# Hybrid diffusion step on one core: modulation with the conditioning columns stationary, prompt routing inside the latent q and k stage, prompt steps 2.95 gathers apart

## The reference

```
def modulation(cvec, w_ada, b_ada):                 # w_ada: 1024 x 6144 for each layer
    mod = jax.nn.silu(cvec) @ w_ada + b_ada
    return jnp.split(mod[:, None, :], 6, axis=-1)

def trunk_layer(x, mod, lp, l, ctx):
    sh1, sc1, g1, sh2, sc2, g2 = mod
    h = modulate(x, lp['norm1_g'], sh1, sc1)
    y, new_ctx = mixer(h, lp, l, ctx)               # pooling, neighbourhood, conv, differential
    x = x + g1 * y
    h = modulate(x, lp['norm2_g'], sh2, sc2)
    x = x + g2 * peer_ffn(h, ...)
    return x, new_ctx

# peer_ffn, for each token and each of 8 heads:
s = einsum('thpk,hpnk->thpn', qry, sub_keys)        # two rows of 128 scores
s1, i1 = top_k(s[:, :, 0], 16); s2, i2 = top_k(s[:, :, 1], 16)
sc, ci = top_k(all 256 sums s1 + s2, 16)            # "routing": 16 experts of 16384
e, g = expert numbers, softmax(sc)
act = gelu(u_tab[e] . h);  y += (g * act) * v_tab[e]
```

## Time and profile before

| | |
|---|---|
| median of 3 runs | 5567.07 us (5561.44 to 5568.31) |
| profiled execution | 5559.97 us |
| its span | 5558.2 us |
| PE, DVE, ACT, POOL busy | 86%, 60%, 34%, 32% |
| weight load on PE (PEld) | 44% |
| DMA | 1652 MB, mean 297 GB/s |

### The profile page before, as it was taken

One profiled execution on the slowest core, in us unless ns is written; L12 is line 12 of the kernel. 1 busy time (PEld: TensorE's weight loads), 2 busy tenths in 40 slices (PEclk: granted clock), 3 DMA queues, 4 the chain that ended last, 5 costly groups with the idle time before them and its releaser, 6 DMA issues.

```text
span 5558.2 us, 47001 instructions
## 1 busy us (share of the span) xinstructions
PE 4754.9 (86%) x14692; PEld 2460.7 (44%) x14692; DVE 3357.0 (60%) x7181; ACT 1867.9 (34%) x4962; POOL 1760.4 (32%) x1599
## 2 busy tenths in 40 slices
PE   8885999999988778888888789899988777777877
PEld 8684447964434224334554244554334222222222
DVE  0425654147766867766545846577766867667544
ACT  0121023124422334366643311444422333333333
POOL 0200610013222445433333436022322344434432
PEclk9987997579999999999999999999999999999999
DMA  5653221369976999999999923059976999999998
GB/s 178 204 196 96 73 83 59 104 215 349 353 281 258 421 420 410 420 404 384 385 413 420 421 85 106 20 201 348 347 280 233 421 422 421 421 420 416 420 421 359
DMA packets 270202, 1652.11 MB, mean 297 GB/s; under 512 B 31040, under 2 KB 31088, under 8 KB 105472
## 3 DMA queue, kind: packets, MB, share of 16 engines
q0 software_dynamic: 190896, 1365.43, 61.2%
q1 hardware_dynamic: 76032, 276.86, 14.4%
q10 hardware_dynamic: 3024, 6.82, 0.3%
HBM read 1642.16 MB, written 6.82 MB: 297 GB/s over the span
## 4 chain that ended last, share of the span: by engine, by line
PE 43%; DMA 35%; DVE 11%; ACT 7%; issue 3%; POOL 0%; DVEq 0%; ACTq 0%; POOLq 0%
DMA arena<-experts,bsb 26%; PE ps L1619 10%; PE ps L1997 9%; DMA arena<-experts,peidx 9%; PE ps L1609 6%; PE ps L1785 6%; DVE arena L1539 3%; PE ps L1897 2%; PE ps L1875 2%; PE ps L1727 2%; DVE arena L1297 2%; ACT L970 1%; ACT T L974 1%; PE ps L1911 1%; ACT bsb L971 1%
## 5 line engine op out<-in xcount | busy, mean ns | idle before, releaser
L1997 PE MATMUL ps<-arena,T 128*128 128x512 f32 x4096 | 2003.5, 618 | 530.5 <-ACT T L974 529.0
L1539 DVE CUSTOM_DVE_ANT_0 arena<-arena,h_sb 128x1024 f32<-128x1024 f32 x1024 | 1254.2, 1226 | 771.8 <-DMA arena<-experts,bsb 768.0
L631 POOL DMA_INDIRECT arena<-experts,bsb x1024 | 1092.7, 1067 | 1670.3 <-PE ps L1997 1545.9
L1997 PEld LDWEIGHTS ps<-arena,T 128*128 128x128 f32 x4096 | 715.3, 191 | 1736.7 <-ACT T L974 1154.1
L970 ACT ACTIVATE bsb<-T 128x1 f32<-128x1 f32 x1024 | 205.9, 201 | 1321.3 <-DVE T L1539 1320.0
L1619 PE MATMUL ps<-h_sb,wring 128*128 128x128 f32 (+1 forms) x1792 | 509.9, 442 | 96.5 <-DVE h_sb L1334 86.2
L616 POOL DMA_INDIRECT arena<-experts,peidx x256 | 282.2, 1102 | 809.6 <-DVE arena L1297 754.8
L1931 PE MATMUL ps<-h_sb,wring 128*128 128x512 f32 x1024 | 456.9, 599 | 32.8 <-DVE arena L1487 30.3
L974 ACT ACTIVATE T<-ident,bsb 128x128 f32<-128x128 f32 x1024 | 410.9, 401 | 33.5
L1619 PEld LDWEIGHTS ps<-h_sb,wring 128*128 128x128 f32 x1792 | 280.7, 196 | 316.4 <-issue 301.7
L1287 DVE CUSTOM_DVE_ANT_0 arena<-arena,h_sb 128x1024 f32<-128x1024 f32 x256 | 312.6, 1222 | 103.5 <-DMA arena<-experts,peidx 102.6
(11 more groups left out here) (283 smaller groups left out, 4622.9 us busy)
## 6 DMA issues: line engine op xcount, KB each, us to landing
wring<-w SPq DMA_DIRECT2D x528, 512.0 KB, 4.7
arena<-experts,bsb POOLq DMA_INDIRECT x1024, 15.3
bsb<-bias POOLq DMA_DIRECT2D x16, 512.0 KB, 3.9
arena<-subk POOLq DMA_DIRECT2D x4, 1024.0 KB, 7.1
arena<-v_scratch POOLq DMA_DIRECT2D x64, 64.0 KB, 2.1
arena<-experts,peidx POOLq DMA_INDIRECT x256, 7.9
x_sb<-xT POOLq DMA_DIRECT2D x1, 2048.0 KB, 13.7
v_scratch<-arena ACTq DMA_DIRECT2D x8, 256.0 KB, 2.0
```

Source lines behind the costliest of these rows:

```text
L631: gp.indirect_dma_start(rows[:, n % NS, :], None, experts, bass.IndirectOffsetOnAxis(ap=eidx[:, t % 2, i:i + 1], axis=0)).then_inc(row_in[ ...
L1539: v.tensor_tensor_reduce(e, e, htok(t), 1.0, 0.0, ALU.mult, ALU.add, dots[:, t % 2, i:i + 1]).then_inc(dot, 1)
L1997: mm = pe.matmul(ps[:, 6 + half, :], diag[:, n % ND, :], rows[:, n % NS, D + half * 512:D + (half + 1) * 512], start=(i == 0), stop=(i == ...
```

## The change

1. **Modulation.** The conditioning columns become the stationary operand, padded to 32 columns (`csil32`), and the weights move past them, 512 at a time. The chunks of `w_ada` are stored another way (`_row_chunks`): four chunks are one group of 512 output columns, each chunk with a quarter of the rows. The four partial products go to four column groups of the array (partitions 0, 32, 64, 96 of one PSUM bank). ACT copies the bank (`modulation_rows`), and four small matmuls with `pick` (two columns, each with a one for every quarter), add the four quarters and turn the result into columns (`modulation_columns`). There are 12 groups for a layer; those of layer 1 stand at every second nat job.
2. **Prompt routing** of each layer moves into the latent q and k stage of that layer, nine steps behind each `qk_norm`. It has its own scratch and score area. `prompt_gates` and `prompt_soften` go behind the attention.
3. **Spacing.** The steps of the prompt mixer of layer 1 stand 2.95 gathers apart instead of 2.4; the last is at gather 505.

```diff
-NADA = 48
+NADA, ADA_GROUPS = 48, 12
 def gather_of(k):
-    return PAIRS + 12 * k // 5
+    return PAIRS + 295 * k // 100
...
+        pick = sb("pick", [P, 2])
+        lroute, proute = routing(bsb, 256), routing(arena, 26752)
-        pscores = at(arena, 0, 16, NKEYS)
+        pscores = at(arena, 24704, 16, NKEYS)
+        csil32 = at(arena, 28416, KD, 32)
+        mrow = at(arena, 24704, 2, 512)
...
             # ACT
-            act.activation(csil[:], csil[:], ACT.Silu).then_inc(csil_ok, 1)
+            act.activation(csil32[:, :, 0:2], csil[:], ACT.Silu).then_inc(csil_ok, 1)
+            def modulation_rows(l, n):
+                act.wait_ge(ada_row, ADA_GROUPS * l + n + 1)
+                need(act, ada_cols, ADA_GROUPS * l + n - 1)
+                act.activation(mrow[:, n % 2, :], ps[:, 1 + 2 * (n % 2), :], ACT.Copy).then_inc(ada_rows, 1)
...
-            prompt_gates(0)
                 job_out(NJOBS - 1)
+                prompt_gates(l)
...
             # DVE
+            own.link(v.tensor_reduce(pick[:], ident.rearrange("p (q r) -> p r q", r=32)[:, 0:2, :], AX_X, ALU.add))
-            for _ in prompt_route(0):
-                pass
-            prompt_soften(0)
+                routing_steps = prompt_route(l)
                 for n in range(NQ + 1):
                     if n < NQ:
                         qk_mean(n)
                     if n >= 1:
                         qk_norm(n - 1)
+                        for _ in range(9):
+                            next(routing_steps, None)
...
                     job_probs(n)
+                prompt_soften(l)
                 if l + 1 < DEPTH:
                     modulation(l + 1)
...
             # PE
-            def modulation_chunk(l, c):
-                wait_chunk(pe, "A", l, c)
-                for k in range(KD):
-                    mm = pe.matmul(ps[:, 1, 2 * c:2 * c + 2], chunk_of("A", l, c)[:, k * P:(k + 1) * P], csil[:, k, :], ...)
-                mm.then_inc(used("A", l, c), 1)
+            def modulation_group(l, n):
+                need(pe, ada_rows, ADA_GROUPS * l + n - 1)
+                for q in range(4):
+                    wait_chunk(pe, "A", l, 4 * n + q)
+                for kk in range(2):
+                    for q in range(4):
+                        mm = pe.matmul(ps[32 * q:32 * q + 32, 1 + 2 * (n % 2), :], csil32[:, 2 * q + kk, :], chunk_of("A", l, 4 * n + q)[:, kk * 512:(kk + 1) * 512], ...)
+                        if kk:
+                            mm.then_inc(used("A", l, 4 * n + q), 1)
+                for q in range(4):
+                    wait_used(pe, "A", l, 4 * n + q)
+                pe.sem_inc(ada_row, 1)
+            def modulation_columns(l, n):
+                pe.wait_ge(ada_rows, ADA_GROUPS * l + n + 1)
+                for i in range(4):
+                    c = 4 * n + i
+                    mm = pe.matmul(ps[:, 5, 2 * c:2 * c + 2], mrow[:, n % 2, i * P:(i + 1) * P], pick[:], start=True, stop=True)
+                mm.then_inc(ada_cols, 1)
```

More of the change, by code:

```diff
@@ L642, in _ @@
             act.wait_ge(ctab, 16)
-            act.activation(csil[:], csil[:], ACT.Silu).then_inc(csil_ok, 1)
+            act.wait_ge(csil_zero, 1)
+            act.activation(csil32[:, :, 0:2], csil[:], ACT.Silu).then_inc(csil_ok, 1)
[3 more added lines that the diff above has]
+                act.activation(mrow[:, n % 2, :], ps[:, 1 + 2 * (n % 2), :], ACT.Copy).then_inc(ada_rows, 1)
+            for n in range(ADA_GROUPS):
+                modulation_rows(0, n)
             def prompt_mixer(l):
@@ L895, in map_exp @@
                                    bias=st[:, o + i:o + i + 1], accum_out=st[:, o + 2 + i:o + 3 + i]).then_inc(exp_done, 1)
+                ada_job = {NDIFF + 2 * n + 2: n for n in range(ADA_GROUPS)}
                 def job_out(n):
@@ L1005, in _ @@
                     y_out(t)
[L1006 to L1008 removed]
+                if l + 1 == DEPTH:
                     give(NL - 1, NL)
@@ L1027, in modulation, with route @@
                 v.sem_inc(ada_ok, 1)
-            def route(l, sc, eidx_out, gate_out, idx_sem, top_sem, gate_free):
+            def route(l, r, sc, eidx_out, gate_out, idx_sem, top_sem, gate_free):
+                top, topf, topi, csc, ci, abf, sel, half = [r[n] for n in ("top", "topf", "topi", "csc", "ci", "abf", "sel", "ef")]
                 cand = sc.rearrange("p n c -> p (n c)").rearrange("p (h a b) -> p h a b", h=GH, a=TOPK)
@@ L1101, in route, with soften @@
                 yield
[L1103 removed]
+            def soften(r, gates, gexp_sem, n, ok_sem):
                 v.wait_ge(gexp_sem, n)
+                total, inv = r["sums"][:, 0, :], r["sums"][:, 1, :]
                 g3 = gates.rearrange("p (h k) -> p h k", h=GH)
[L1107 to L1109 removed]
+                own.link(v.tensor_reduce(total, g3, AX_X, ALU.add))
+                own.link(v.reciprocal(inv, total))
+                v.tensor_tensor(g3, g3, inv.unsqueeze(2).broadcast_to([P, GH, TOPK]), ALU.mult).then_inc(ok_sem, 1)
             def prompt_mixer(l):
@@ L1430, in _ @@
                         conv_norm()
+                for _ in routing_steps:
+                    pass
                 def map_max(m):
@@ L1567, in _ @@
                     at_dot = gates_at(t)
-                    if t == 0:
-                        steps = itertools.chain(latent_route(0, 1), latent_route(1, 0), latent_route(1, 1))
-                    elif t + 1 < NL:
-                        steps = itertools.chain(latent_route(t + 1, 0), latent_route(t + 1, 1))
-                    else:
-                        steps = prompt_route(l + 1) if later else iter(())
+                    groups = [(0, 1), (1, 0), (1, 1)] if t == 0 else [(t + 1, 0), (t + 1, 1)] if t + 1 < NL else []
+                    steps = itertools.chain(*[latent_route(*tg) for tg in groups])
                     for i in range(PAIRS):
@@ L1576, in _ @@
                         dot_row(t, i)
-                        if t + 1 < NL or here > gather_of(PSTEPS - 1) + 3:
-                            for _ in range((2, 1 + i % 2, 1 + i % 2, 3)[t]):
-                                next(steps, None)
+                        for _ in range(1 + i % 2 if t else 2):
+                            next(steps, None)
                         if i - 4 in at_dot:
@@ L1590, in _ @@
                             next(mixer)
-                    for _ in steps:
-                        assert t == NL - 1
+                    assert next(steps, None) is None
                 assert next(mixer, None) is None
@@ L1760, in prompt_mixer @@
                     yield
-            for c in range(NADA):
-                modulation_chunk(0, c)
             pe.wait_ge(ada_ok, 1)
+            for n in range(ADA_GROUPS):
+                modulation_group(0, n)
+                if n:
+                    modulation_columns(0, n - 1)
+            modulation_columns(0, ADA_GROUPS - 1)
+            pe.wait_ge(ada_ok, 2)
             for _ in prompt_mixer(0):
@@ L1904, in _ @@
                         job_values(n - 1)
-                    if l + 1 < DEPTH and n >= NDIFF:
-                        for c in range(3 * (n - NDIFF) // 2, 3 * (n - NDIFF + 1) // 2):
-                            modulation_chunk(l + 1, c)
+                    if l + 1 < DEPTH and n > NDIFF and (n - NDIFF) % 2:
+                        if (n - NDIFF) // 2 < ADA_GROUPS:
+                            modulation_group(l + 1, (n - NDIFF) // 2)
+                        if 0 < (n - NDIFF) // 2 <= ADA_GROUPS:
+                            modulation_columns(l + 1, (n - NDIFF) // 2 - 1)
                     pe.wait_ge(pd_ready, NJOBS * l + n + 1)
@@ L1915, in _ @@
                 if l + 1 < DEPTH:
-                    pe.wait_ge(ada_ok, l + 2)
+                    pe.wait_ge(ada_ok, l + 3)
                 for h in range(4):
@@ L2035 @@
     order = (0, 2, 1, 3)
-    stream, small, rowg, lamrow = [_col_chunks(a["w_ada"][l]) for l in range(DEPTH)], [], [], []
+    stream, small, rowg, lamrow = [_row_chunks(a["w_ada"][l]) for l in range(DEPTH)], [], [], []
     for l in range(DEPTH):
```

52 lines of the change are left out of this document (23 added, 29 removed).

## The result

The changed kernel takes 5324.04 us (median of 4, 5315.08 to 5333.51) beside 5567.69 us for the kernel before on the same chip: ratio 0.9565, 95% interval 0.9541 to 0.9588. Forecast were 5288 us and faster; the gain is 244 us instead of 279, inside the range.

The account below looks back on a forecast made before the run. Gathers were the largest item in the chain, with PE alone on modulation, DVE alone on routing, and nat jobs at 1.2 GHz. Terms -69 - 40 - 160 - 20 + 10 = -279 us gave 5288 us, range 5230 to 5370.

Parts of the forecast that it names:

- rival 1: Modulation groups: column groups run one after the other at 2.4 GHz, 6.87 us a group; 5352 us in all; chance 22%.
- Rival 4: Both q and k stages: DVE, not PE, sets them, steps stretched to 1.3, and spacing brings nothing; 5332 us; chance 12%.
- A: Layer 0's modulation at the start: becomes bound by the chunk ring, ending at 114 instead of 182.6 us; -69 us.
- B: Layer 0's prompt routing: PE's gap before the latent projections shrinks 49.8 us, q and k holds cost 10; -40 us.
- E: Layer 1: routing in its q and k stage +10, softening at the layer boundary -1, gates behind attention +1; +10 us.
- C: Layer 1's modulation among layer 0's nat jobs: twelve groups at 2.4 GHz, stage about 113 us; -160 us with later waits.
- Rival 2: Nat stage of layer 0: groups run side by side but the clock stays at 1.2 GHz; 5363 us; chance 8%.
- D: Layer 0's expert stage: wider spacing of prompt mixer steps raises the gather rate; -20 us, bounds 0 and -37.

Follow-up runs that it names:

- second fit: Changed kernel with routing steps placed by time budgets per unit, none in unit 6, leftovers behind layer 0's nat jobs and layer 1's last unit; 5304.33 us, ratio 0.9523.
- in pairs: Against the kernel that waits for each chunk by itself: a group's chunks 0 and 1 are finished before chunk 2 begins; 5279.82 us, ratio 0.9498.
- both finds: Changed kernel with each chunk waited for by itself and released early, plus routing steps fitted a third time in both layers; 5250.65 us, ratio 0.9445.

## Why the forecast was right, and where it was off

**What bounds, and the sign: right.** Every stage that was named moved, and those that were not named moved by at most 3.4 us. The four column groups run side by side at 1.92 us (forecast 1.72); one column group costs 7.03 and rival 1 is out. That rival was itself priced too low: I gave it 5352 us, and the kernel that has it takes 5414. Its cycle at the start was 10.1 us at 2.4 GHz, not 9.2, and 11.8 on average, since most of its groups ran in part at 1.2 GHz (7.03 to 9.66 us). The Trainium skill ("TensorE: Matmul & The Clock Gate", Part 3) has 2.38x for three column tiles, 0.79 of ideal; here four reached 7.03/1.92 = 3.7, 0.92 of ideal, and the measurement decides. Rival 4 is out too: the 1024-wide routing steps took 1.21 to 1.23 us, as before (1.22 to 1.23), one of them (at 610.11 us) with POOL at work beside it, and the spacing brought its share.

**A, the start: right, 6 us short.** The cycle is 8.5 us, the end 119.9 instead of 114. I took the middle of a warm and a cold start; it was cold (0.66). That slots released together make the wait is shown from both sides: five slots cost 15.3 us, and waiting for each chunk by itself, which releases the first ones earlier, gives 26.5 back.

**B, the gap: right to 0.3 us** (49.7), and shown again by undoing it (48.8).

**B and E, the hold in the q and k stages: the mechanism right, the size off.** I had 10 us in each layer and measured 15.4 and 19.0. The step that failed is "PE is held 4 us after unit 8 and 6 us at the last two transposes". PE's last two waits were 3.65 + 6.33, 6 us more than before, as forecast, and behind unit 8 it waited 2.43. What I had not seen is another 3.66 at 631.79 us, ahead of unit 8's steps. In the timeline VectorE comes late to the centring of the convolution in unit 6, behind nine steps, ScalarE waits for that, and the next mean waits for ScalarE; in the second fit, with no step in unit 6, this wait is gone. In layer 1 pieces of the projection behind a wait ran at the lower clock too (8.1 and 8.7 us for 7.03). That the place of the steps does it is shown: fitted to the idle time, with 11.3 us of them ahead of the first two units, the same 140 steps cost 1.3 and 2.6 us.

**C, the nat jobs: the step that failed.** The forecast -162 came as -136. The sum, 12 groups at 3.1 us + 0.5 for chunks, holds at 2.4 GHz: groups with their columns take 3.3 us, two jobs and a group 7.4 to 7.6 us. The kernels in which the clock stayed up (in pairs, both finds) had the stage at 112 us; the forecast of 113, less the 5 us ahead of the first group, is 108, and waiting for chunks makes up the rest (9.7 us in pairs, where the sum had 6). What failed is the premise that 2.4 GHz holds, taken from layer 1's jobs, where nothing waits for a chunk. In the profile PE waited 2.1, 0.8 and 1.5 us for chunks, each time the pieces behind the wait went over to 1.2 GHz, the stage had a clock of 0.77, and its last eight jobs cost 13 us more for it. That the clock is the loss is shown by the stage's table. Rival 2, the stage at 1.2 GHz, thus came true in part. That idle time before a group brings the clock down is shown as far as this: in the eight kernels with 4.6 to 14.2 us of it the clock was 0.74 to 0.90, in the five with 0 to 1.4 us 0.91 to 1.00, with the tail at 1.00 in all five. The small columns and the narrow stationary tiles, rival 2's reasons, are excluded as causes by themselves: the kernel in pairs has all of both at 1.00. It is no law: the same code had its tail at 1.2 GHz in one profile and at 2.4 in another, more waiting did not mean a lower clock, the kernel with one column group had two slow groups (8.2 and 8.5 us for 7.05) with no wait for a chunk at all, and why an execution takes the one or the other stays open.

**D: right** (-19.6 for -20; 15.6 by undoing the spacing alone). The forecast's own sign of it, no window under 400 GB/s, was not met: behind the first, two of the 50 us windows had 372 and 398, for 333 at worst before.

In the profiled executions -279 was forecast and -228 measured. Of these 51 us 26 are C's, 14 the two holds', 6 A's, and 5 the rest together, mostly small stages that I had left at nothing. The medians differ from the forecast by 36: the profiled execution of the changed kernel is of the longer pair of the four, 8 us over its median, and that of the kernel before was 8 us under its own.

## What to carry to other kernels

Price an accelerated piece with the wait that it uncovers: when a group is nearly four times as fast, what feeds it sets the pace, and the cheapest cure may be to wait for each buffer by itself and so release it earlier (more buffers were not tried). A step moved under other work costs nothing only where that engine idles in that very unit, so place steps by their time against the idle time that the trace shows, not by equal counts. When a forecast relies on the higher TensorE clock, look for short waits in the stage; here 1.5 us of waiting stood ahead of 13 us lost to the clock.

## What the runs showed of the hardware

- Four column groups of 32 columns in float32 take 1.92 us for eight 512-column matmuls at 2.4 GHz, 7.03 us in one column group.
- The order of issue doesn't matter for it: in pairs, or with two matmuls of one column group in a row, a group takes 1.94 us when its data is there. In the trace the first instructions of all four column groups start within 0.04 us, ahead of instructions of the first column group that stand before them in the list.
- The granted clock of the same 106 matmuls was 0.50 in one execution and 1.00 in another (30.5 and 17.5 us), with no other difference in the code ahead of them.
- At the start, groups in one column group (7.03 us at 2.4 GHz) had a granted clock of 0.88, those side by side 0.66 where all four chunks were waited for together, and 0.95 to 1.00 where each was waited for by itself.
